# Keys of the selected and window branches: transposed two groups at a time, doubled over the partitions at the copy out of PSUM

## The reference

```
h  = rmsnorm(x, norm1)
z  = h @ w_in                        # split: z_rx, z_ry, z_q, z_kc, z_vc, z_ks, z_vs, z_kw, z_vw, ...
xr = rg_lru(causal_conv(z_rx, ...))  # recurrent branch
q  = rmsnorm(z_q  per head of 64,  q_norm)        # 16 heads
kc = rmsnorm(compress(z_kc ...), k_norm[0])       # hidden layer of 256, gelu
vc = compress(z_vc ...)
k_s = rmsnorm(z_ks per group of 64, k_norm[1])    # 4 groups of 4 heads: keys of the selected branch
k_w = rmsnorm(z_kw per group of 64, k_norm[2])    # 4 groups: keys of the window branch
o   = gate0 * attn(q, kc, vc) + gate1 * attn(q, k_s, v_s) + gate2 * attn(q, k_w, v_w)
x   = x + (sig * (xr*gelu(z_ry)) @ w_rg_out + sig * o @ w_nsa_out) @ w_o
x   = x + (silu(h2 @ w_gate) * (h2 @ w_up)) @ w_down,   h2 = rmsnorm(x, norm2)
```

## Time and profile before

| | us |
|---|---|
| three runs, median (lowest to highest) | 490.8 (489.51 to 490.82) |
| profiled execution, its own time | 488.86 |
| its span, first to last instruction | 487.1 |
| PE busy | 477.9 (98%) |
| DVE busy | 353.8 (73%) |
| ACT busy | 280.4 (58%) |
| POOL busy | 15.1 (3%) |

### The profile page before, as it was taken

How to read it: one execution, slowest core, us unless ns; L and a number is a source line. 1 busy time by engine, 2 the same in 40 slices (tenths; PEclk the granted TensorE clock), 3 DMA queues, 4 the chain that set the end, 5 groups by cost and what they waited for, 6 DMA issues and landing times.

```text
span 487.1 us, 7342 instructions
## 1 busy us (share of the span) xinstructions
PE 477.9 (98%) x2805; PEld 412.0 (85%) x2805; DVE 353.8 (73%) x625; ACT 280.4 (58%) x448; POOL 15.1 (3%) x25
## 2 busy tenths in 40 slices
PE   5999999999999999999999999999999999999997
PEld 5998998688999778877787888888888888888885
DVE  3899799789896877757763767787777777754332
ACT  5755886765566996566763335745555445453320
POOL 2000200211000000000000000000000000000000
PEclk9999999999899999999999999999999999999999
DMA  8745868524224245433234362565555455554402
GB/s 312 271 160 207 330 256 311 174 87 173 87 86 174 87 173 188 159 124 137 104 155 168 98 253 87 192 242 180 191 204 203 174 172 186 200 218 174 174 0 86
DMA packets 12689, 84.73 MB, mean 174 GB/s; under 512 B 1520, under 2 KB 1520, under 8 KB 2928
## 3 DMA queue, kind: packets, MB, share of 16 engines
q1 hardware_dynamic: 11952, 82.32, 46.4%
q0 software_dynamic: 272, 1.05, 0.7%
q10 hardware_dynamic: 432, 0.91, 0.5%
HBM read 83.22 MB, written 1.05 MB: 173 GB/s over the span
## 4 chain that ended last, share of the span: by engine, by line
PE 95%; DVE 2%; DMA 1%; issue 1%; ACT 0%; SPq 0%; DVEq 0%
PE bank L1089 19%; PE bank L1091 19%; PE bank L1090 19%; PE bank L1123 16%; PE bank L1126 8%; PE bank L1209 2%; PE bank L1245 2%; PE bank L1427 1%; DMA raw<-stream_dram 1%; PE bank L1218 1%; PE bank L1293 1%; PE bank L1252 1%; PE bank L1249 1%; PE bank L1228 1%; DVE xs L993 1%
## 5 line engine op out<-in xcount | busy, mean ns | idle before, releaser
L667 DVE TENSOR_TENSOR w_lo<-raw,w_hi 128x2048 fp32r<-128x2048 f32 x72 | 164.8, 2290 | 52.4 <-ACT w_hi L370 52.0
L370 ACT ACTIVATE w_hi<-raw 128x2048 fp32r<-128x2048 f32 x72 | 137.8, 1916 | 46.3 <-PE bank L1091 46.3
L1123 PE MATMUL bank<-h_hl,w_hi 128*128 128x512 f32 x336 | 84.3, 393 | 0.0
L1123 PEld LDWEIGHTS bank<-h_hl,w_hi 128*128 128x128 f32 x336 | 60.5, 189 | 10.7
L1089 PE MATMUL bank<-w_hi,h_hl 128*128 128x512 f32 x160 | 63.7, 398 | 0.0
L1091 PE MATMUL bank<-w_hi,h_hl 128*128 128x512 f32 x160 | 62.5, 391 | 0.0
L1090 PE MATMUL bank<-w_lo,h_hl 128*128 128x512 f32 x160 | 62.5, 390 | 0.0
L1089 PE MATMUL bank<-w_hi,act 128*128 128x512 f32 x152 | 60.0, 395 | 0.0
L1091 PE MATMUL bank<-w_hi,act 128*128 128x512 f32 x152 | 59.3, 390 | 0.0
L1090 PE MATMUL bank<-w_lo,act 128*128 128x512 f32 x152 | 59.3, 390 | 0.0
L1126 PEld LDWEIGHTS bank<-h_hl,w_lo 128*128 128x128 f32 x336 | 45.8, 190 | 3.2
(11 more groups left out here) (228 smaller groups left out, 706.9 us busy)
## 6 DMA issues: line engine op xcount, KB each, us to landing
raw<-stream_dram SPq DMA_DIRECT2D x72, 1024.0 KB, 4.8
w<-stream_dram SPq DMA_DIRECT2D x4, 1024.0 KB, 8.8
raw<-stream_dram SPq DMA_DIRECT2D x2, 512.0 KB, 7.4
xs<-x_dram POOLq DMA_DIRECT2D x1, 1024.0 KB, 5.5
out_dram<-xs SPq DMA_DIRECT2D x4, 256.0 KB, 2.0
xs<-x_dram ACTq DMA_DIRECT2D x1, 512.0 KB, 5.2
xs<-x_dram SPq DMA_DIRECT2D x1, 512.0 KB, 5.0
scr<-small_dram ACTq DMA_DIRECT2D x1, 320.0 KB, 8.6
```

What stands on the lines that cost most here:

```text
L370: sc.activation(w_hi[:, i % HL, :], raw[:, i % RAW, :], ACT.Copy).then_inc(hi_ready, 1)
L667: ve.tensor_tensor(w_lo[:, i % HL, :], raw[:, i % RAW, :], f(w_hi[:, i % HL, :]), ALU.subtract).then_inc(lo_ready, 1)
L1123: ins = pe.matmul(acc(u + mt)[:, :], w_hi[:, s, c:c + P], a_hl[:, k, :, :].rearrange("p x s -> p (x s)"), start=k == 0, stop=k == KC - 1)
```

## The change

`kn` holds each block once, 512 columns for each token half. A transpose now takes two groups (128 channels) at a time: group 2v comes out on partitions 0 to 63 and group 2v+1 on 64 to 127 of bank v, 8 transposes into two banks. ACT and DVE then copy each group out twice, once to partitions 0 to 63 and once to 64 to 127, in instructions of 64 partitions: `src` is the group's half in the bank, `e` the half that is written. The uses of the `misc` ring behind `kT` move up by two numbers.

```diff
-("kT", 4)
+("kT", 2)
@@ ACT, i == FIRST["kk"] + 4
                     for g in range(GROUPS):
-                        m = MISC["kT"] + g
+                        m = MISC["kT"] + g // 2
+                        src = slice(64 * (g % 2), 64 * (g % 2) + 64)
                         sc.wait_ge(misc_done, misc_count(m))
-                        for b in range(2):
-                            ins = sc.activation(k_hh[:, g, b * S:(b + 1) * S], misc(m)[:, b * S:(b + 1) * S], ACT.Copy,
-                                                scale=prm[:, KN + 1 + b:KN + 2 + b])
+                        for e in range(2):
+                            for b in range(2):
+                                ins = sc.activation(k_hh[64 * e:64 * e + 64, g, b * S:(b + 1) * S], misc(m)[src, b * S:(b + 1) * S],
+                                                    ACT.Copy, scale=prm[src, KN + 1 + b:KN + 2 + b])
                         ins.then_inc(evac_hi, 1)
@@ DVE, i == FIRST["kk"] + 3
-                        ve.tensor_tensor(kn[:, t, :].rearrange("p (c e d) -> p c e d", c=8, e=2),
-                                         kz[:, t, :].rearrange("p (c d) -> p c d", c=8).unsqueeze(2).broadcast_to([P, 8, 2, DH]),
-                                         rs_wide(NORM_K, t, [P, 8, 2, DH]), ALU.mult).then_inc(kn_ready, 1)
+                        ve.tensor_tensor(kn[:, t, 0:512].rearrange("p (c d) -> p c d", c=8),
+                                         kz[:, t, :].rearrange("p (c d) -> p c d", c=8),
+                                         rs_wide(NORM_K, t, [P, 8, DH]), ALU.mult).then_inc(kn_ready, 1)
@@ DVE, i == FIRST["kk"] + 4
                     for g in range(GROUPS):
-                        m = MISC["kT"] + g
+                        m = MISC["kT"] + g // 2
+                        src = slice(64 * (g % 2), 64 * (g % 2) + 64)
                         ve.wait_ge(evac_hi, g + 1)
-                        for b in range(2):
-                            ins = ve.scalar_tensor_tensor(out=k_ll[:, g, b * S:(b + 1) * S], in0=misc(m)[:, b * S:(b + 1) * S],
-                                                          scalar=prm[:, KN + 1 + b:KN + 2 + b],
-                                                          in1=f(k_hh[:, g, b * S:(b + 1) * S]), op0=ALU.mult, op1=ALU.subtract)
-                        ins.then_inc(misc_free[m % 4], 1)
+                        for e in range(2):
+                            for b in range(2):
+                                dst = slice(64 * e, 64 * e + 64)
+                                ins = ve.scalar_tensor_tensor(out=k_ll[dst, g, b * S:(b + 1) * S], in0=misc(m)[src, b * S:(b + 1) * S],
+                                                              scalar=prm[src, KN + 1 + b:KN + 2 + b],
+                                                              in1=f(k_hh[src, g, b * S:(b + 1) * S]), op0=ALU.mult, op1=ALU.subtract)
+                        if g % 2 == 1:
+                            ins.then_inc(misc_free[m % 4], 1)
@@ PE, i == FIRST["kk"] + 3
-                    for g in range(GROUPS):
-                        m = MISC["kT"] + g
+                    for v in range(2):
+                        m = MISC["kT"] + v
                         wait_misc_free(pe, m)
                         for b in range(2):
                             for t in range(T2):
-                                c = (4 * b + g) * P
+                                c = (2 * b + v) * P
                                 ins = pe.transpose(misc(m)[:, b * S + t * P:b * S + (t + 1) * P], kn[:, t, c:c + P], ident[:, :])
                         ins.then_inc(misc_done, 1)
```

More of the change, by code:

```diff
@@ L58 @@
 USE_RY = [USE["ry0"], USE["ry1"], USE["ry1"] + 1, USE["ry3"]]
-MISC_ORDER = [("xT", 4), ("ng", 1), ("ngT", 1), ("kT", 4), ("hid", 1), ("kcn", 1), ("qTa", 2), ("vrep", 1), ("qTb", 2), ("att", 4 * HEADS), ("mT", 4), ("hT2", 4)]
+MISC_ORDER = [("xT", 4), ("ng", 1), ("ngT", 1), ("kT", 2), ("hid", 1), ("kcn", 1), ("qTa", 2), ("vrep", 1), ("qTb", 2), ("att", 4 * HEADS), ("mT", 4), ("hT2", 4)]
 MISC = {}
```

## The result

The changed kernel is slower: median 491.86 us (490.13 to 494.15, 19 executions) against 489.81 (488.90 to 491.01, 19 executions) for the kernel before. The ratio is 1.0035, with a 95% interval of 1.0022 to 1.0048. The profiled execution took 490.13 us (span 488.4) where that of before took 488.86; the fastest executions of the two series are 1.23 us apart. Four executions in the experiments that took 530 to 1229 us (three of before, one of experiment 3) are left out of all numbers.

The account below looks back on a forecast made before the run. PE was taken to bound the kernel, 95% of 487.1 us; DVE's 3.92 - 0.94 = 2.98 us lateness, plus 0.13, minus 1.97 reserve, gave 1.14 later: 490.8 + 1.1 = 491.9 us. Range 489.9 to 493.6, the forecast's own 491.2 to 492.7.

Parts of the forecast that it names:

- The transposes: PE's key transposes, 16 becoming 8: 0.88 us off the chain; keeping it as a gain, 489.9 us, had chance 0.06.
- The start of the keys on DVE: DVE's key copies can start at 66.13 us instead of 67.07, 0.94 earlier, after narrower scaling and one split.
- DVE's sixteen: DVE's key copies, eight of 128x256 becoming sixteen of 64x256: 7.06 us, 3.92 more, half overlapping; chance 0.52.
- the ends: DVE's key copies: all overlap, 6.28 us, 491.2 total, chance 0.12; none overlaps, 7.84 us, 492.7 total, chance 0.20.
- ACT's sixteen: ACT's key copies, eight becoming sixteen: 6.9 us, 4.0 more, ending at about 70.7 us, hidden by gaps behind them.
- The meeting: Compression's hidden layer: second gathering on DVE ends at 86.96, PE waits about 2.0 us and starts at 87.09, 1.14 later.
- the forecast sum: Whole kernel: DVE 2.98 us late plus 0.13 signalling minus 1.97 reserve, 1.14 us later; median 490.8 + 1.1 = 491.9.
- the rival on the clock: PE's stall at 85 us lowers the granted clock: 1.7 us on top of 1.14, 493.6 us; chance 0.10.
- The row that I held against it: Early in the kernel, PE idle 2.48 us up to 10.17 while clock stayed 1.00: evidence against a stall costing clock.
- The warning that the prediction takes from the Trainium skill: On PE: avoid idle gaps between bursts of matmuls; the prediction noted the 2.48 us gap did not cost the clock.
- slower by over 0.3%: Outcome for the whole kernel beyond about 1.5 us: chance 0.36, against same 0.59 and faster 0.05.
- A sign that I named wrongly: Profile after, before the hidden layer: new PE idle time of about 2.0 us, put down to DVE.

Follow-up runs that it names:

- experiment 3: The changed kernel with 16 idle transposes on PE in the stall before the hidden layer, run twice: medians 490.35 and 490.42 us, ratios 1.0029 and 1.0030.
- 1: The changed kernel with its 8 transposes, but ACT and DVE copying as before in 8 instructions of 128x256 each: 488.37 us, ratio 0.9969 to before.
- 9: The changed kernel with each group copied once, 8 instructions of 64x256 per engine, and four DMAs filling the other half: 488.64 us, ratio 0.9975 to before.
- experiment 5: The kernel before with only ACT's and DVE's copies split, each 128x256 into two of 64x256: 492.76 us, ratio 1.0055.
- experiment 4: The changed kernel with DVE's k_ll copies moved behind the second gathering and split_lo(13), ACT's copies unmoved: 497.24 us, ratio 1.0153.
- 6: The changed kernel unaltered, measured again in three runs: 491.98, 490.41 and 491.98 us.
- experiment 8: The changed kernel with three more DVE instructions, about 1.4 us, before the second gathering to lengthen PE's stall: 495.14 us, ratio 1.0120.
- 7: The changed kernel with 8 ordinary 512-column matmuls on PE in the stall before the hidden layer: 490.98 us, ratio 1.0033.
- experiment 2: The changed kernel with each of the 8 transposes issued twice: 490.99 us median, 490.18 in the profiled execution, ratio 1.0040.

## Why the prediction was right

- *The transposes:* 0.88 us forecast, 0.87 on the chain after. Where nothing takes it back (1, 9), the fastest executions are 0.76 and 0.72 below before's and the medians 1.2 and 1.1.
- *The start of the keys on DVE:* 66.13 forecast, 65.97 measured (that execution is 0.15 us earlier from 56 us on).
- *DVE's sixteen:* 7.06 forecast, 7.20 measured, and the alternation of 0.39 and 0.49 that the choice between the ends rested on is there as 0.40 and 0.49 (in experiment 5 too, where nothing crosses the halves). The change of the written half alone, of which no row of before told, holds an instruction back. In the Trainium skill, "VectorE: DVE Perf Modes", section "Two Vector instructions with no wait between them", the start quadrants (groups of 32 partitions) of inputs and output both count; this trace agrees, by starts 0.48 apart where only the output changes.
- *ACT's sixteen:* 6.9 forecast, 6.79 measured, and hidden. I had room for it in ACT's own followers and did not see how near it was: without DVE's copies it would have held DVE by 5.2 us (4).
- *The meeting:* gathering at 86.96 forecast, 87.08 measured; hidden layer at 87.09 and 87.18; stall about 2.0 and 2.17; the profiled execution 490.0 and 490.13. Its difference to before is 1.27 us where 1.14 was forecast.
- *What was too small:* the difference of the medians is 2.05 us, by the ratio 0.35% or 1.7 us, where 1.1 was forecast. The forecast of 491.9 met 491.86 partly by luck, as it started from a median of three, 490.8, that 19 executions put at 489.81. With all executions of the table the fastest are 1.33 us apart and the medians 2.2, so the forecast sum accounts for the first and about 0.9 us is on top. The term that was mis-sized is the rival on the clock. Its price was right (1.7 us forecast, 1.63 in the execution caught in 6). Wrong was to treat it as a case that is there or not, at a chance of 0.10: it comes in a part of the executions. That such executions make up the 0.9 us is argued from the groups and from that one profile, not shown. The row that I held against it, PE idle up to 10.17 us with the clock at 1.00, was one execution; in the one of experiment 5 the clock did fall behind that same place. The warning that the prediction takes from the Trainium skill, "TensorE: Matmul & The Clock Gate", stands in its section "Why this matters for your kernels". The traces of experiments 4, 5 and 6 agree with it, by falls behind 4.92, 2.1 and 2.18 us of idle time (the last two gaps are shorter than those that the page warns of), and that of experiment 8 does not, with 1.00 behind 3.52. With this seen, "slower by over 0.3%" would have had more than "same"; I had it at 0.36 against 0.59.
- *A sign that I named wrongly:* the wait was to be put down to DVE. The profile says `issue`, and names DVE's L916 only for the short idle times of 0.38 us (3) and 0.26 us (7); in experiment 4 it says `issue` for 0.44 us.

**What stays open.** No profile caught an execution at 493 or above, so where the second costly fall lies there is not shown; a fall at the start and one behind the stall would add up to it. Nor is it explained why 6 of 33 executions stand there with the stall filled to 0.4 us. A rival is untested: that it is not PE's idle time but the later start of all that follows, which filling the stall does not change, that puts a fall where it costs more.

## What to carry to other kernels

Work taken off the busiest engine (here 0.88 us of PE) is worth its size only up to the reserve of the result that it waits for next. Work out that reserve (here 1.97 us, shown by no view) before giving another engine 3 us of work, and look behind the first late chain for the next one. Where an operand is needed on both halves of the partitions, doubling it by elementwise copies costs a full instruction for each half and an overlap at each change of half. If there is time, a DMA can do it beside the rest, as four of 256 KB did here. Judge a stall of PE by many executions, since its price in clock shows in some of them only.

## What the runs showed of the hardware beyond that

- ACT holds an instruction back at a change of half as DVE does: its sixteen take 6.79 us, and they start by turns 0.36 to 0.38 and 0.47 to 0.49 apart, where eight on all partitions took 0.36 each. The first four:

```profile
63.63 0.45 ACT L513 ACTIVATE act<-bank,prm 64x256 fp32r<-64x256 f32 x1
63.99 0.46 ACT L513 ACTIVATE act<-bank,prm 64x256 fp32r<-64x256 f32 x1
64.46 0.47 ACT L513 ACTIVATE act<-bank,prm 64x256 fp32r<-64x256 f32 x1
64.83 0.46 ACT L513 ACTIVATE act<-bank,prm 64x256 fp32r<-64x256 f32 x1
```

- The fall of the clock near 130 us, which the earlier trace rows has, cost nothing where it stands in the two executions compared here. The profiled execution of experiment 2 had none there, that of the first run of experiment 3 had it; their stretches:

```profile
124.00:140.00 16.00, 14.58 (x121) 14.05 (x120) 14.59 (x34) 9.01 (x22) 0.00 (x0) 1.00 0.23 77
```

```profile
124.00:140.00 16.00, 16.00 (x121) 15.50 (x120) 14.60 (x34) 8.90 (x22) 0.00 (x0) 0.89 0.26 75
```

Both do the same 121 matmuls and 34 instructions of DVE in these 16 us, and the executions took 490.18 and 490.15 us. PE waited 2.3 us for ACT at 140.9 us in the first and 0.8 in the second: the stretch is bound by DVE and ACT, so here a slower PE only shortened its own wait.
